# Three rotary units moved from the projection stage into the key-search score stage, and the search's state put in PSUM

## The chip, the cores and the metric

The kernel runs on one core of a Trainium2 chip. The metric is the device time of one execution in microseconds; the median of the runs counts. The engines are PE (TensorE), DVE (VectorE), ACT (ScalarE), POOL (GpSimd) and SP (which here only starts DMAs).

## What is computed

The reference is a first block (three gated recurrences and a feed-forward layer) and then a second block of two identical attention layers (`DEPTH_2 = 2`) on a sequence of 1024 tokens and a width of 1024. Only the second block is touched. Of one of its layers this matters:

```python
h = jnp.einsum('bsd,de->bse', x, w_in)          # all projections at once
sq = rope(sq...); sk = rope(sk, pos)            # queries and key of the sparse attention
iq = rope(iq...); ik = rope(ik, pos)            # queries (8 heads) and key of the index
sc = jnp.einsum('bqhd,bsd->bqhs', qib, ki)
idx_score = jnp.einsum('bqhs,bqh->bqs', jax.nn.relu(sc), wib)
idx_score = where(causal, idx_score, -inf)      # then top-k: the 256 best keys of every query
```

The sparse attention then looks only at each query's 256 best keys. The other projections (`fox` queries and keys, the gate, the `diff` queries and keys with rotary embedding, the values) do not depend on the search.

## The kernel before, in words

A **unit** is one 128-column slice of the projection, computed transposed into a PSUM pair (two banks, 128x1024): `unit_products` (L357) issues 48 matmuls, that is 2 halves x 8 row blocks `k` x `three_products` (L341, lines 344 to 346), since each f32 operand is split in a rounded part and a rest. POOL makes the split of the weights for each unit (a CAST, then a subtract of the full width). Some units are rotary: DVE takes the pair out twice (times cos into the destination, times sin into `rot`), ACT's queue starts four DMAs that turn the halves (`turn_halves`, L368) into `partner`, and DVE adds `partner` to the destination.

Each stage is an `nc.Block`: every engine has its own in-order program, semaphores order them, and all engines meet at the end of the block. One layer runs, in this order:

1. `product_stage` "pa" (L375): eight rotary units, three for `SQ` (sparse queries and key) and five for `IQ` (index queries and key), with four PSUM pairs in rotation, then a **wide** part: 332 columns of token-major products in all eight banks, of which bank pair `t//2` may be written once the unit that used it last has been taken out (`scaled`). ACT makes a rounded copy `SQ_high`, POOL the rest `SQ_rest`. DMA loads go through six slots.
2. `index_stage` (L1840): scores. For each of the eight query tiles `t` (with n = 128(t+1) keys) and each pair of the eight heads (32 **steps** in all, 64 heads `j`), PE multiplies two heads, each with 64 rows, into one of four PSUM pairs (L1866); ACT applies relu into `R`, four slots (L1878); DVE multiplies by the head's weight and adds up (L1894, L1891), and after each `t` takes the largest absolute value (L1898) and adds the causal mask (L1899). No units run here.
3. `search_stage` (L1999). DVE runs `TopK.search` (L1934): 32 rounds of bisection. A round is `mid` = `lo` + step (L1958), three counts on DVE (L1961) beside three on ACT (L1930), `keep` = count <= need (L1965), `lo` += keep x step (L1966). Then `TopK.select` (L1975) picks exactly 256 keys. Meanwhile PE computes 20 units over four PSUM pairs: 12 that ACT copies out between its counts (`COPIED`), then 8 rotary units that DVE takes out after it has finished the search and the selection. PE may start unit u when unit u-4 has been taken out. After the units comes a wide part of 512 columns in the eight banks. PE begins with five spin matmuls (L338) that keep it busy until the first weights are split.
4. The three attention stages and `finish_stage`.

The order of work on each engine is written out by hand; there is no planner.

Of the kernel before, what the change touches and what calls it, by code (L numbers as in the profile page):

```python
# [16 lines left out]
P = 128  # L17
# [357 lines left out]
def product_stage(kit, tag, XT, rest, items, ropes, rope, place, rot, partner, halves, wide):  # L375
# [9 lines left out]
    (products, taken, dve_own, scaled, rope_in, split, rounded, bank_done, wide_taken, high_done, low_done) = (  # L385
        kit.sem(f"{tag}_{n}") for n in ("products", "taken", "dve_own", "scaled", "rope_in", "split", "rounded",
                                        "bank_done", "wide_taken", "high_done", "low_done"))
    with ExitStack() as mem:
# [5 lines left out]
        with nc.Block() as block:  # L394
# [33 lines left out]
            @block.scalar  # L428
            def _(act):
                for n in range(U + 1):  # L430
# [5 lines left out]
                    if 0 < n <= len(halves):  # L436
                        plain, high, _ = halves[n - 1]
                        act.wait_ge(taken, n)
                        act.activation(high, plain, ACT.Copy).then_inc(high_done, 1)
# [5 lines left out]
            def _(pool):  # L445
                for i, (_, width) in enumerate(items):
# [7 lines left out]
                    if 0 <= i - 3 < len(halves):  # L454
                        plain, high, low = halves[i - 3]
                        pool.wait_ge(high_done, i - 2)
                        pool.tensor_tensor(low, plain, high.bitcast(FP32), ALU.subtract).then_inc(low_done, 1)
# [1382 lines left out]
def index_stage(kit, IQ, VS, IS, AM, causal, prepare):  # L1840
# [3 lines left out]
    scored, bent, added, done, own_d = (kit.sem(f"ix_{n}") for n in ("scored", "bent", "added", "done", "own_d"))  # L1844
    H = 8
    SLOTS = 4
    with ExitStack() as mem:
        R = sbuf(nc, mem, "ix_R", [P, SLOTS, S])
        with nc.Block() as block:
            @block.sync  # L1850
            def _(sp):
                prepare.load(sp)

            @block.tensor
            def _(pe):
                for t in range(NT):
                    n = P * (t + 1)
                    for h in range(0, H, 2):
                        j = t * H + h
                        if j >= SLOTS:  # L1860
                            pe.wait_ge(bent, j + 1 - SLOTS + 1)
                        for c in range(0, n, HALF):
                            e = min(n, c + HALF)
                            for m in range(2):
                                rows = slice(64 * m, 64 * m + 64)
                                last = pe.matmul(kit.pair((j + m) % SLOTS)[:, c:e], IQ[rows, h // 2, t * P:(t + 1) * P],  # L1866
                                                 IQ[rows, 4, c:e], start=True, stop=True)
                                if e == n:
                                    last.then_inc(scored, 1)

            @block.scalar
            def _(act):
                for j in range(NT * H):
# [4 lines left out]
                    act.activation(R[:, j % SLOTS, 0:n], kit.pair(j % SLOTS)[:, 0:n], ACT.Relu).then_inc(bent, 1)  # L1878

            @block.vector  # L1880
            def _(dve):
                own = Own(dve, own_d)
                for t in range(NT):
                    n = P * (t + 1)
                    out = IS[:, keys_at(t):keys_at(t) + n]
                    for h in range(H):
# [9 lines left out]
                        ins.then_inc(added, 1)  # L1896
                    dve.wait_ge(added, (t + 1) * H)
# [5 lines left out]
class TopK:  # L1903
# [5 lines left out]
    def __init__(self, kit, mem, IS, AM, MB, B, R, causal):  # L1909
# [6 lines left out]
        self.mid, self.cnt, self.need, self.keep, self.lo, self.hi = (  # L1916
            small(n, [P, 2 * N]) for n in ("mid", "cnt", "need", "keep", "lo", "hi"))
# [17 lines left out]
    def search(self, dve):  # L1935
# [4 lines left out]
        lo, hi, mid, keep, steps, top = self.lo, self.hi, self.mid, self.keep, self.steps, self.top  # L1940
# [4 lines left out]
        own(dve.tensor_scalar(lo, steps[:, 0:1].to_broadcast([P, 2 * N]), -1.0, None, ALU.mult))  # L1945
# [11 lines left out]
        for i in range(BISECTIONS):  # L1957
            dve.tensor_scalar(mid, lo, steps[:, i:i + 1], None, ALU.add).then_inc(self.act_mid, 1)  # L1958
# [7 lines left out]
            own.then(dve.scalar_tensor_tensor(lo, keep, steps[:, i:i + 1], lo, ALU.mult, ALU.add))  # L1966
# [32 lines left out]
def search_stage(kit, XT, rest, items, topk, staged, partner, rot, fox, GATE, FQD, rope, DQD, DV):  # L1999
# [5 lines left out]
    n_pairs, SLOTS, PARTS, RING, TURNS = 4, 2, 2, len(staged), 2  # L2005
# [7 lines left out]
    (rounded, split, products, copied, rope_in, scaled, added, dve_own, bank_done, wide_taken) = (  # L2013
        kit.sem(f"tk_{n}") for n in ("rounded", "split", "products", "copied", "rope_in", "scaled", "added",
                                     "dve_own", "bank_done", "wide_taken"))
    with ExitStack() as mem:
# [5 lines left out]
        with nc.Block() as block:  # L2022
# [10 lines left out]
            def _(pool):  # L2033
                for i, (_, width) in enumerate(items):
# [6 lines left out]
                    pool.tensor_tensor(w2, w, w1.bitcast(FP32), ALU.subtract).then_inc(split, 1)  # L2041

            @block.tensor
            def _(pe):
                spin(kit, pe, 3, 5)
# [9 lines left out]
                for k in range(KT):  # L2055
                    i = U + k
                    pe.wait_ge(split, i + 1)
                    for t in range(NT):
                        if k == 0 and t % 2 == 0:
                            pe.wait_ge(scaled, ROPES - n_pairs + t // 2 + 1)  # L2060
# [5 lines left out]
                        elif t == NT - 1:  # L2066
# [3 lines left out]
            def _(act):  # L2070
# [24 lines left out]
                for t in range(NT):  # L2095
                    act.wait_ge(bank_done, t + 1)
# [754 lines left out]
def layer(kit, l, XD, XT, REST, DQ, C, LAM, OM, GATE, FQD, DQD, half_size, d):  # L2851
# [23 lines left out]
    items = [(w_feat[m], S) for m in range(8)]  # L2875
    items += rows_of(w_tok, 0, 332)
    dst = [SQ[:, j, :] for j in range(3)] + [IQ[:, j, :] for j in range(5)]
    ropes = [(dst[m], QK_SCALE if m < 2 else IDX_SCALE if 3 <= m < 7 else 1.0) for m in range(8)]
# [3 lines left out]
                  rot=MB[:, 0:4 * S].bitcast(FP32).rearrange("p (a n) -> p a n", a=2),  # L2882
                  halves=[(SQ[:, m, :], SQ_high[:, m, :], SQ_rest[:, m, :]) for m in range(3)], wide=wide)
    IS = flat[:, 0:KEYS]
    index_stage(kit, IQ, VS, IS, AM, causal, prepare)
    index.close()
    DV = ends.enter_context(nc.sbuf_tensor("DV", [P, NT, 512], FP32, side="right"))[:, :, :]
    with ExitStack() as mem:
# [5 lines left out]
        search_stage(kit, XT, REST, items, topk, staged, slots_of(0, 2), slots_of(2, 4), [QK_SCALE] * 2 + [1.0] * 2, GATE, FQD, rope, DQD, DV)  # L2894
# [146 lines left out]
```

## Time and profile before

| | |
|---|---|
| median of 3 runs | 3120.19 us (3117.55 to 3122.45) |
| the profiled execution | 3115.68 us, its span 3114.0 us |
| PE busy | 2840.1 us, 91% of the span |
| DVE busy | 1677.7 us, 54% |
| ACT busy | 983.8 us, 32% |
| POOL busy | 791.7 us, 25% |

The times of the trace count from the start of the span. The two layers lie at 1349 to 2216 us and from 2234 us on. A matmul of 512 columns is shown with 0.39 us, though the next one starts 0.23 us later: they overlap, so the distance between starts is what a matmul costs. "Idle" in brackets is the time the engine stood still before the row, and behind the arrow what released it.

### The profile page before, as it was taken

What the parts mean: (1) busy time and instruction counts of PE and PEld (TensorE: products, weight loads), DVE (VectorE), ACT (ScalarE), POOL (GpSimd) and SP (SyncE); (2) the same over time, 40 slices, a digit from 0 to 9 for tenths busy, and PEclk for the clock granted to TensorE, in tenths of its full rate; (3) what the DMA queues carried; (4) which work ended last, traced back from release to release, by engine and by line L of the source; (5) the groups of instructions that cost most, each with busy time, mean ns of one, the idle gap of its engine ahead of it and who ended that gap; (6) DMA issues with size and microseconds to landing.
All of it is one profiled execution on the core that took longest, in us unless ns stands there. A gap on an engine that the chain in (4) does not pass through costs nothing. (4 is left out here: it accounts for less than half of the span.)

```text
span 3114.0 us, 39179 instructions
## 1 busy us (share of the span) xinstructions
PE 2840.1 (91%) x14936; PEld 2311.2 (74%) x14936; DVE 1677.7 (54%) x2806; ACT 983.8 (32%) x1911; POOL 791.7 (25%) x510
## 2 busy tenths in 40 slices
PE   6999888989999999989699889989897898999988
PEld 4768678778888888868388778777684686778767
DVE  5170476534223233333999545675446998265855
ACT  3150454220000000111564034563105560244751
POOL 2233103223233333323033261003130332340021
PEclk9999899999999999999999999999899999999999
DMA  3101002111111111131122420004320224300032
GB/s 113 35 34 49 1 1 99 48 41 38 51 58 38 50 59 48 55 122 47 41 89 89 139 92 1 1 13 165 131 64 3 96 87 123 141 1 1 1 135 95
DMA packets 83146, 194.07 MB, mean 62 GB/s; under 512 B 15488, under 2 KB 34448, under 8 KB 81936
## 3 DMA queue, kind: packets, MB, share of 16 engines
q1 hardware_dynamic: 71056, 153.78, 14.6%
q10 hardware_dynamic: 11904, 37.76, 3.9%
q8 instruction: 123, 2.02, 0.3%
q14 instruction: 63, 0.52, 0.1%
HBM read 141.18 MB, written 33.55 MB: 56 GB/s over the span
## 5 line engine op out<-in xcount | busy, mean ns | idle before, releaser
L344 PE MATMUL psum<-H,tk_W 128*128 128x512 f32 x640 | 250.9, 392 | 23.1 <-DVE OM L2124 22.9
L344 PE MATMUL psum<-H,ffn_W 128*128 128x512 f32 x672 | 262.9, 391 | 4.8 <-DVEq L1716 3.1
L346 PE MATMUL psum<-H,ffn_W 128*128 128x512 f32 x672 | 262.4, 390 | 0.0
L345 PE MATMUL psum<-H,ffn_W 128*128 128x512 f32 x672 | 262.4, 390 | 0.0
L345 PE MATMUL psum<-H,tk_W 128*128 128x512 f32 x640 | 250.3, 391 | 0.0
L346 PE MATMUL psum<-H,tk_W 128*128 128x512 f32 x640 | 250.0, 391 | 0.0
L1930 ACT ACTIVATE MB<-OM,tk_mid 128x384 bf16<-128x384 f32 (+2 forms) x192 | 157.2, 819 | 120.7 <-DVE tk_mid L1958 119.9
L1961 DVE TENSOR_SCALAR_CACHE_REDUCE MB<-OM,tk_mid 128x512 bf16<-128x512 f32 (+2 forms) x192 | 184.3, 1010 | 2.3
L1483 POOL CAST ffn_W<-ffn_W 128x1024 fp32r<-128x1024 f32 (+1 forms) x77 | 65.1, 845 | 471.4 <-PE psum L346 469.6
L2039 POOL CAST tk_W<-tk_W 128x1024 fp32r<-128x1024 f32 (+1 forms) x56 | 53.6, 958 | 512.1 <-PE psum L346 361.0
L1697 DVE TENSOR_SCALAR ffn_Y<-ffn_G,ffn_par 128x1024 f32<-128x1024 f32 x21 | 21.1, 1004 | 288.6 <-ACT ffn_G L1670 288.6
L1670 ACT ACTIVATE ffn_G<-psum 128x1024 f32<-128x1024 f32 x21 | 21.6, 1029 | 445.6 <-PE psum L346 445.6
L344 PEld LDWEIGHTS psum<-H,tk_W 128*128 128x128 f32 x640 | 121.0, 189 | 50.1 <-issue 23.7
L1485 POOL TENSOR_TENSOR ffn_W<-ffn_W,ffn_W 128x1024 fp32r<-128x1024 f32 (+1 forms) x77 | 152.6, 1982 | 6.2
L344 PEld LDWEIGHTS psum<-H,ffn_W 128*128 128x128 f32 x672 | 126.8, 189 | 32.3 <-POOLq L1556 3.5
L346 PEld LDWEIGHTS psum<-H,ffn_W 128*128 128x128 f32 x672 | 126.7, 189 | 26.7
L345 PEld LDWEIGHTS psum<-H,ffn_W 128*128 128x128 f32 x672 | 126.8, 189 | 26.1
L2715 POOL TENSOR_TENSOR fin_W_rest<-fin_W 128x2048 fp32r<-128x2048 f32 x4 | 22.4, 5604 | 462.8 <-ACT fin_W L2685 462.8
L346 PEld LDWEIGHTS psum<-H,tk_W 128*128 128x128 f32 x640 | 121.0, 189 | 25.4
L345 PEld LDWEIGHTS psum<-H,tk_W 128*128 128x128 f32 x640 | 121.0, 189 | 25.3
L344 PE MATMUL psum<-ffn_W,ffn_PR 128*128 128x512 f32 x336 | 131.1, 390 | 0.0
L346 PE MATMUL psum<-ffn_W,ffn_PR 128*128 128x512 f32 x336 | 130.8, 389 | 0.0
(442 smaller groups left out, 7219.7 us busy)
## 6 DMA issues: line engine op xcount, KB each, us to landing
tk_W<-in_w_feat SPq DMA_DIRECT2D x40, 512.0 KB, 3.6
ffn_W<-in_ffn_w_gate SPq DMA_DIRECT2D x21, 512.0 KB, 3.5
ffn_W<-in_ffn_w_val SPq DMA_DIRECT2D x21, 512.0 KB, 3.5
ffn_W<-in_ffn_w_down SPq DMA_DIRECT2D x42, 256.0 KB, 2.6
OM<-in_w_feat SPq DMA_DIRECT2D x16, 512.0 KB, 7.7
OM<-MB ACTq DMA_DIRECT2D x64, 128.0 KB, 2.4
GATE<-OM ACTq DMA_DIRECT2D x16, 512.0 KB, 2.9
OM<-OM ACTq DMA_DIRECT2D x64, 128.0 KB, 2.9
```

What stands on the lines that cost most here:

```text
L344: pe.matmul(out, a1, b1, start=start, stop=False)
L345: pe.matmul(out, a1, b2, start=False, stop=False)
L346: return pe.matmul(out, a2, b1, start=False, stop=stop)
L1483: pool.tensor_copy(w1, w).then_inc(self.rounded, 1)
L1485: pool.tensor_tensor(w2, w, w1.bitcast(FP32), ALU.subtract).then_inc(self.split, 1)
L1670: act.activation(G[:, j % 2, 2:2 + S], kit.pair(j % 2), ACT.Copy).then_inc(gate_out, 1)
L1697: own.then(dve.tensor_scalar(y, x[:, 2:2 + S], par[:, 2, j:j + 1], par[:, 3, j:j + 1], ALU.mult, ALU.add))
L1930: last = act.activation(self.MB[:, self.keys(t)], self.IS[:, self.keys(t)], ACT.Sign, scale=-1.0, bias=self.mid[:, 3 + n:4 + n], accum_out ...
L1961: own(dve.tensor_scalar(MB[:, self.keys(t)], IS[:, self.keys(t)], mid[:, n:n + 1], 0.0, ALU.is_lt, ALU.add, accum_out=self.cnt[:, n:n + 1]))
L2039: pool.tensor_copy(w1, w).then_inc(rounded, 1)
L2715: pool.tensor_tensor(w_part(W2, c, 0), w_part(W, c, 0), w_part(W1, c, 0).bitcast(FP32), ALU.subtract).then_inc(w_low_pool, 1)
```

## The change

- `product_stage` "pa" computes only the five `IQ` units. Its wide part waits at each bank pair for the last of the five units that used it; `SQ_high` and `SQ_rest` are no longer made here.
- `index_stage` also computes the three `SQ` units. SP loads their weights (two slots) and the cos/sin table, POOL splits them, PE cuts each unit in 16 **chunks** of three matmuls and issues some after each step (more in later tiles, none in the last four steps), all into the fourth PSUM pair; scores use three pairs. DVE takes each unit out after the second head of the step in which it ends (`rotate`, which waits for `products`), ACT's queue starts the turning DMAs four heads later, DVE adds the partner eight heads later. PE may begin unit u only when DVE has taken out unit u-1 (`scaled`).
- `search_stage` has three PSUM pairs for units; the last pair's bank 7 holds the bisection's `need` and `low` (the running lower bound, copied to `lo` in SBUF once the rounds are over). The wide part starts with banks 4 to 7. POOL now makes both `SQ_high` (in ACT's place) and `SQ_rest`, behind its splits 3, 4 and 5.

```diff
 def product_stage(...)                       # pa
-                            pe.wait_ge(scaled, U - n_pairs + t // 2 + 1)
+                            pe.wait_ge(scaled, [u for u in range(U) if u % n_pairs == t // 2][-1] + 1)
...
-                        act.activation(high, plain, ACT.Copy).then_inc(high_done, 1)
...
-                        pool.tensor_tensor(low, plain, high.bitcast(FP32), ALU.subtract).then_inc(low_done, 1)
 def index_stage(...)
-    SLOTS = 4
+    H, SLOTS, PAIRS, PARTS, UNIT_PAIR, CHUNKS = 8, 4, 3, 2, 3, 2 * KT
+    share = [j // 4 + 1 for j in range(STEPS - 4)]
+    upto = [min(CHUNKS * U, CHUNKS * U * sum(share[:j + 1]) // sum(share)) for j in range(STEPS)]
+    last_step = [[j for j in range(STEPS) if upto[j] >= CHUNKS * (u + 1)][0] for u in range(U)]
...
+                for i, (src, _) in enumerate(items):
+                    if i >= PARTS:
+                        sp.wait_ge(split, i - PARTS + 1)
+                    sp.dma_start(W[:, i % PARTS, :], src).then_inc(w_in[i % PARTS], 16)
+                    if i == 0:
+                        sp.dma_start(table, rope).then_inc(rope_in, 16)
...
+                    if i >= PARTS:
+                        pool.wait_ge(products, i - PARTS + 1)
+                    pool.tensor_copy(w1, w).then_inc(rounded, 1)
+                    pool.wait_ge(rounded, i + 1)
+                    pool.tensor_tensor(w2, w, w1.bitcast(FP32), ALU.subtract).then_inc(split, 1)
...
+                def chunk(n):
+                    u, c, k = n // CHUNKS, n % CHUNKS // KT, n % KT
+                    if n % CHUNKS == 0:
+                        pe.wait_ge(split, u + 1)
+                        if u:
+                            pe.wait_ge(scaled, u)
+                    w1, w2 = (a[:, u % PARTS, k * P:(k + 1) * P] for a in (W1, W2))
+                    at = slice(c * HALF, (c + 1) * HALF)
+                    last = three_products(pe, kit.pair(UNIT_PAIR)[:, at], w1, w2, XT[:, k, at], rest[:, k, at],
+                                          k == 0, k == KT - 1)
...
+                for step in range(STEPS):
+                    scores(step)
+                    for n in range(upto[step - 1] if step else 0, upto[step]):
+                        chunk(n)
...
+                    for u in range(U):
+                        if j == 2 * last_step[u] + 1 + SLOTS:
+                            act.wait_ge(scaled, u + 1)
+                            if u:
+                                act.wait_ge(turned, u)
+                            turn_halves(act, partner, rot, swapped)
...
+                        for u in range(U):
+                            if j == 2 * last_step[u] + 1:
+                                rotate(u)
+                            if j == min(2 * last_step[u] + 1 + 2 * SLOTS, NT * H - 1):
+                                add_partner(u)
 class TopK
+        self.need, self.low = (kit.psum[:, 7, 8 * n:8 * n + 2 * N] for n in range(2))
...
-            dve.tensor_scalar(mid, lo, steps[:, i:i + 1], None, ALU.add).then_inc(self.act_mid, 1)
+            dve.tensor_scalar(mid, low, steps[:, i:i + 1], None, ALU.add).then_inc(self.act_mid, 1)
...
             own.then(dve.tensor_tensor(keep, self.cnt, self.need, ALU.is_le))
-            own.then(dve.scalar_tensor_tensor(lo, keep, steps[:, i:i + 1], lo, ALU.mult, ALU.add))
+            own.then(dve.scalar_tensor_tensor(low, keep, steps[:, i:i + 1], low, ALU.mult, ALU.add))
+        own.then(dve.tensor_copy(lo, low))
 def search_stage(...)
-    n_pairs, SLOTS, PARTS, RING, TURNS = 4, 2, 2, len(staged), 2
+    n_pairs, SLOTS, PARTS, RING, TURNS = 3, 2, 2, len(staged), 2
+    WIDE_ORDER = (4, 5, 6, 7, 0, 1, 2, 3)
...
+                    if 0 <= i - 3 < len(halves):
+                        plain, high, low = halves[i - 3]
+                        pool.tensor_copy(high, plain).then_inc(high_done, 1)
+                        pool.wait_ge(high_done, i - 2)
+                        pool.tensor_tensor(low, plain, high.bitcast(FP32), ALU.subtract).then_inc(low_done, 1)
```

## Rows read from the trace of the kernel before

**Rows 1.** Busy by stretch, layer 1, "pa" and scores: PE, PEld, DVE, ACT, POOL, clock

```profile
1349.60:1473.00 123.40, 122.44 (x586) 103.31 (x586) 33.99 (x24) 6.28 (x10) 45.87 (x35) 0.99 0.30 88
1473.00:1539.00 66.00, 40.33 (x193) 16.44 (x192) 57.70 (x80) 41.44 (x66) 0.00 (x0) 0.91 0.01 3
```

**Rows 2.** Timeline, DVE in the score stage: start, us, line, operation, count

```profile
1475.00 3.09 DVE L1891 SCALAR_TENSOR_TENSOR OM<-ix_R,VS,OM 128x128 f32<-128x128 f32 x7
...
1516.61 8.69 DVE L1891 SCALAR_TENSOR_TENSOR OM<-ix_R,VS,OM 128x896 f32<-128x896 f32 x7
...
1538.41 0.29 DVE L1899 TENSOR_TENSOR OM<-OM,CONST 128x128 f32<-128x128 f32 x1
```

**Rows 3.** Timeline, PE in the score stage and at the search stage's start

```profile
1473.79 0.71 PE L1866 MATMUL psum<-IQ 64*128 64x128 f32 x8 [0.79 <-PEq L394]
...
1499.94 1.56 PE L1866 MATMUL psum<-IQ 64*128 64x512 f32 x8 [1.15 <-ACT ix_R L1878]
...
1526.46 1.99 PE L1866 MATMUL psum<-IQ 64*128 64x512 f32 x8 [0.52 <-ACT ix_R L1878]
1539.26 7.02 PE L338 MATMUL psum<-CONST 128*128 128x512 f32 x10 [10.81 <-PEq L1849]
```

**Rows 4.** Timeline, end of DVE's select and PE's restart, layer 1; PE's in layer 2

```profile
1730.34 1.21 DVE L2124 SCALAR_TENSOR_TENSOR OM<-psum,tk_table 128x1024 f32<-128x1024 f32 x1
...
1731.70 0.77 PE L344 MATMUL psum<-H,tk_W 128*128 128x512 f32 x1 [10.83 <-DVE OM L2124]
...
1735.56 0.39 PE L344 MATMUL psum<-H,tk_W 128*128 128x512 f32 x1
...
2616.08 0.76 PE L344 MATMUL psum<-H,tk_W 128*128 128x512 f32 x1 [12.04 <-DVE OM L2124]
```

**Rows 5.** PE alone by stretch: stretch, busy, granted clock, DMA share, GB/s

```profile
1731.70:1733.00 1.30, 1.30 (x3) 0.50 0.22 50
```

**Rows 6.** Timeline, POOL's first split in each stage and two later ones

```profile
1357.08 1.04 POOL L451 CAST pa_W<-OM 128x1024 fp32r<-128x1024 f32 x1 [0.31 <-DMA OM<-in_w_feat]
...
1542.99 1.04 POOL L2039 CAST tk_W<-tk_W 128x1024 fp32r<-128x1024 f32 x1 [75.61 <-DMA tk_W<-in_w_feat]
...
1655.73 1.04 POOL L2039 CAST tk_W<-tk_W 128x1024 fp32r<-128x1024 f32 x1 [7.35 <-PE psum L346]
...
1666.61 1.04 POOL L2039 CAST tk_W<-tk_W 128x1024 fp32r<-128x1024 f32 x1 [7.36 <-PE psum L346]
```

**Rows 7.** Timeline, rounds of the search on DVE, with one POOL row

```profile
1541.76 0.22 DVE L1958 TENSOR_SCALAR tk_mid<-tk_lo,tk_steps 128x6 f32<-128x6 f32 x1
...
1547.48 2.44 DVE L1958 TENSOR_SCALAR tk_mid<-tk_lo,tk_steps 128x6 f32<-128x6 f32 x1
...
1547.51 2.39 POOL L2041 TENSOR_TENSOR tk_W<-tk_W 128x1024 fp32r<-128x1024 f32 x1
...
1553.42 0.23 DVE L1958 TENSOR_SCALAR tk_mid<-tk_lo,tk_steps 128x6 f32<-128x6 f32 x1
...
1557.14 0.23 DVE L1958 TENSOR_SCALAR tk_mid<-tk_lo,tk_steps 128x6 f32<-128x6 f32 x1
...
1684.26 0.23 DVE L1966 SCALAR_TENSOR_TENSOR tk_lo<-tk_keep,tk_steps,tk_lo 128x6 f32<-128x6 f32 x1
```

**Rows 8.** Timeline, a wide DVE operation of the selection and POOL beside it

```profile
1711.35 2.39 POOL L2041 TENSOR_TENSOR tk_W<-tk_W 128x1024 fp32r<-128x1024 f32 x1
...
1711.67 3.02 DVE L1990 SCALAR_TENSOR_TENSOR OM<-OM,tk_lo,MB 128x896 bf16<-128x896 f32 x1
```

**Rows 9.** Groups of DVE instructions by form: a small one that reads PSUM

```profile
L2462 DVE TENSOR_REDUCE df_nmax<-psum 128x1 f32<-128x128 f32 x16 | 3.9, 285 | 2.6 <-PE psum L2391 2.6
```

**Rows 10.** Timeline, PE from 64-row to 128-row matmuls in an attention stage

```profile
1923.06 0.40 PE L2139 MATMUL psum<-FQ_high,FQ_rest 64*128 64x512 f32 x2
1923.38 0.39 PE L2221 MATMUL psum<-FB,pickb 128*128 128x512 bf16 x1
```

**Rows 11.** Timeline, ACT's queue starting the four turning DMAs of a unit

```profile
1739.44 2.45 ACTq L372 DMA_DIRECT2D OM<-OM  x4
```

More of the change, by code:

```diff
@@ L372, in turn_halves, with product_stage @@
         act.dma_start(partner[dst, :], rot[src, :]).then_inc(done, 16)
-def product_stage(kit, tag, XT, rest, items, ropes, rope, place, rot, partner, halves, wide):
+def product_stage(kit, tag, XT, rest, items, ropes, rope, place, rot, partner, wide):
     nc = kit.nc
@@ L1854, in _ @@
             @block.tensor
             def _(pe):
[L1856 to L1869, printed above, removed]
+                def chunk(n):
[8 more added lines that the diff above has]
+                                          k == 0, k == KT - 1)
+                    if n % CHUNKS == CHUNKS - 1:
+                        last.then_inc(products, 1)
@@ new lines, in scores @@
+                def scores(step):
+                    t, h = step * 2 // H, step * 2 % H
+                    n, j = P * (t + 1), 2 * step
+                    if j + 1 >= PAIRS:
+                        pe.wait_ge(bent, j + 1 - PAIRS + 1)
+                    for c in range(0, n, HALF):
+                        e = min(n, c + HALF)
+                        for m in range(2):
+                            rows = slice(64 * m, 64 * m + 64)
+                            last = pe.matmul(kit.pair((j + m) % PAIRS)[:, c:e], IQ[rows, h // 2, t * P:(t + 1) * P],
+                                             IQ[rows, 4, c:e], start=True, stop=True)
+                            if e == n:
+                                last.then_inc(scored, 1)
@@ L1882, in _, with rotate, add_partner @@
                 own = Own(dve, own_d)
+                def rotate(u):
+                    dst, scale = ropes[u]
+                    out = kit.pair(UNIT_PAIR)
+                    dve.wait_ge(products, u + 1)
+                    if u == 0:
+                        dve.wait_ge(rope_in, 16)
+                    else:
+                        dve.wait_ge(swapped, 64 * u)
+                    own(dve.scalar_tensor_tensor(dst, out, scale, cos, ALU.mult, ALU.mult))
+                    dve.scalar_tensor_tensor(rot, out, scale, sin, ALU.mult, ALU.mult).then_inc(scaled, 1)
+                def add_partner(u):
+                    dst = ropes[u][0]
+                    dve.wait_ge(swapped, 64 * (u + 1))
+                    own.wait()
+                    dve.tensor_tensor(dst, dst, partner, ALU.add).then_inc(turned, 1)
                 for t in range(NT):
@@ L1939, in search @@
         own = Own(dve, self.own_d)
-        lo, hi, mid, keep, steps, top = self.lo, self.hi, self.mid, self.keep, self.steps, self.top
+        hi, mid, keep, steps, top = self.hi, self.mid, self.keep, self.steps, self.top
+        low, lo = self.low, self.lo
         own.then(dve.tensor_reduce(top, AM[:, T0:NT], AX.X, ALU.max))
@@ L1944, in search @@
         own.then(dve.tensor_scalar(steps[:, 0:1], top, 2.0, None, ALU.mult))
-        own(dve.tensor_scalar(lo, steps[:, 0:1].to_broadcast([P, 2 * N]), -1.0, None, ALU.mult))
+        own(dve.tensor_scalar(low, steps[:, 0:1].to_broadcast([P, 2 * N]), -1.0, None, ALU.mult))
         for b in range(5):
@@ L2893, in layer @@
         items += rows_of(w_tok, 332, 844)
-        search_stage(kit, XT, REST, items, topk, staged, slots_of(0, 2), slots_of(2, 4), [QK_SCALE] * 2 + [1.0] * 2, GATE, FQD, rope, DQD, DV)
+        search_stage(kit, XT, REST, items, topk, staged, slots_of(0, 2), slots_of(2, 4),
+                     [(SQ[:, m, :], SQ_high[:, m, :], SQ_rest[:, m, :]) for m in range(3)], [QK_SCALE] * 2 + [1.0] * 2, GATE, FQD, rope, DQD, DV)
     gates = ExitStack()
```

67 lines of the change are left out of this document (36 added, 31 removed).

## The prediction, made before the changed kernel was run

> **What bounds the kernel now.** I began with the busy shares of the small table: PE is the bound in most stages, so PE work is worth moving only to where PE waits. The busy times by stretch show such a place: in the score stage's 66 us DVE is busy 57.7 and PE 40.3 [rows 1], and DVE's timeline there runs without a gap, a head of one tile taking from 0.44 us (3.09 / 7) at t = 0 to 1.24 (8.69 / 7) at t = 6, about 0.133 more per t [rows 2]. DVE ends at 1538.70; PE has been done since 1528.5 [rows 2, 3]. The second place is inside the search stage, found in the timeline around PE's longest waits: after 16 units PE stands 10.83 us in layer 1 and 12.04 in layer 2, until DVE, done with the selection, has taken out the first rotary unit [rows 4]. It restarts at a granted clock of 0.50, the lower of its two levels [rows 5], after 10.8 us of idling: nine matmuls take 3.86 us where nine at 0.227 take 2.04 [rows 4]. So DVE's search and selection set when the last units run. A unit costs PE 10.88 us, the distance of two POOL splits that each wait for one [rows 6], and a chunk of three matmuls 10.88 / 16 = 0.68.
>
> **Search state in PSUM.** The three small operations take about 0.2 us each, but one that meets a POOL instruction lasts until POOL is done: `mid` took 2.44 us from 1547.48 while POOL's subtract ran from 1547.51 to 1549.90 [rows 7]. A round that meets none takes 1557.14 - 1553.42 = 3.72; 32 of them 119.0. The search took 1684.49 - 1541.76 = 142.7 [rows 7]. If the operations no longer meet POOL, DVE is done 23.7 us earlier per layer. A wide operation with two SBUF operands also waits (3.02 us at 1711.67, about 2.1 of it behind POOL's subtract [rows 8]), so the selection keeps its collisions; it slides by 23.7 us against splits that come each 10.88, and I leave its length as it is. Price of PSUM operands: a small operation of 128 columns out of PSUM takes 0.285 us [rows 9], one within SBUF 0.29 [rows 2]: nothing. For a small write into PSUM no row exists; bounds: 0, and 0.065 per operation. I take 0, since rows 9 and 2 agree to 5 ns.
> The Trainium skill ("SBUF — State Buffer", Who interferes with whom) says that DVE shares a second port pair with GpSimd, and that an instruction with at most one SBUF input, outside the two-port modes, does not contend; by this rule all three new forms escape. The Trainium skill speaks against the change in "VectorE: DVE Perf Modes" (The TRN2 errata): 120 cycles of fixed cost out of PSUM against 58 from SBUF, an estimated 0.065 us each, 6.2 us per layer over 96 operations; the trace, with 0.285 against 0.29, disagrees. By it the sum would be about 10 us less favourable.
>
> **Three pairs instead of four.** PE now stops after 15 units instead of 16. In layer 1 it gets there at 1731.70 - 10.83 - 10.88 = 1710.0; DVE has released it at 1731.55 - 23.7 = 1707.9. Layer 2: 2593.2 against 2592.2 [rows 4, 6]. So neither waits, by 2.1 and 1.0 us. The gain is 10.83 + 12.04 and twice 1.8 for the slow restart: **-26.5 us** for both layers. It is all there is to have: a still faster DVE would find PE busy. POOL's extra work (`SQ_high` and `SQ_rest`, 3 x 3.4 us) fits in its idle 7.35 us per unit [rows 6]; it would cost if it met small operations still held. ACT's copies come, as now, between its counts.
>
> **Units out of "pa".** -3 x 10.88 = -32.6 us per layer on PE, which is busy for 122.4 of the stage's 123.4 us [rows 1]. The wide part now finds its first pair just finished by unit 4 and waits for DVE's two operations of 1.2 us: +2.4. SQ's rounding there was beside PE: nothing.
>
> **Units into the score stage.** PE's own work: scores of a step take 1.99 - 0.28 = 1.71 us at t = 7 and 0.213 less per t (1.56 at t = 5) [rows 3], 31 us in all, and 32.6 of chunks: 63 us, as much as the stage is long. So it can't be hidden whole. I follow DVE through it:
> - The first chunk sits behind step 2, with all later scores queued behind it. In the search stage the first CAST starts 3.7 us after PE's first matmul and the split is done after 7.2 [rows 3, 6]; the second follows at once, table or not (0.31 us of waiting in "pa" [rows 6]). Here: 1481.0, and POOL's second subtract holds DVE to 1484.6. Head 6 started at 1477.2 [rows 2]: **+7.4**. A clock dip like that of rows 5 hits PE, not DVE, here.
> - Unit 0 ends in step 15. Its end releases POOL's third split (3.4 us), which meets the last heads: **+3.4** (0 if it lies in a gap). DVE then takes the unit out: **+2.3**. Chunk 16 waits for that, and the scores of step 16 are queued behind it: chunk 0.68, scores 1.35, a relu of 0.63 (41.44 / 66 [rows 1]), minus 1.0 of DVE's reduce: **+1.8**, and **+1** for a slow clock.
> - Steps 16 to 22 are PE's: 15 chunks and six scores are 17.3 us, plus 14 changes between 64-row and 128-row matmuls at 0.09 (0.32 between starts instead of 0.23 [rows 10]). DVE needs 15.2 for the same heads: **+2.3**, which hides adding the partner.
> - Unit 1 ends in step 22: taken out **+2.3**, refill without cover 0.68 + 1.56 + 0.8: **+3.1**. Steps 23 to 27, by the same reckoning 16.0 against 12.9: **+3.1**. Unit 2: taken out **+2.3**, partner **+1.1**; step 28's scores are not held up.
> The sum is +30.1 us per layer. Lower bound 22 (no collision, little refill, DVE nearly as slow as PE), upper 38 (ACT's queue takes 2.45 us to start four DMAs [rows 11], twice while DVE has no heads in store; slow clocks at both refills). The Trainium skill ("TensorEngine Tiling (Array Packing)", Key Properties) says that a change of tiling mode drains PE; rows 10 show 0.09 us, so the sum stands.
>
> **Sum** per layer for the move: -32.6 + 2.4 + 30.1 = -0.1. Both layers and the search: -26.7 us. The profiled execution took 3115.7, so 3089.0 for one like it; the median of the runs shown is 4.5 us above it: **3093.5 us**. In short, PE work moved from a full stage to one that fills up, while the gain comes from the search's wait.
>
> **Rivals.**
> - *Score stage hides the units.* If DVE stays the bound after the first weights, it grows by 7.4 + 3 x (2.3 + 1.1), less what overlaps, some 16.4 us. Then -13.8 per layer more: -54.1, **3066 us**. For it: PE has 26 us without work there [rows 1]. Against it: unit u+1's chunks wait for DVE with all scores behind them.
> - *Score stage grows more,* by 40 us: late weights, ACT's DMA starts, a halved clock after each wait. Then +9.8 per layer: -6.9, **3113 us**.
> - *Slower: the lock stays.* If the operations still wait for POOL (each reads or writes one SBUF operand, and `mid` still writes to SBUF), the change doesn't do what it says: DVE releases PE when it did, PE stops one unit earlier, at +10.88 us per layer. 21.8 - 0.2: **3142 us**. It decides the sign where the search gets less than 10.9 us shorter per layer. Against it: only POOL's overlap explains why most operations take 0.2 us and a few 2.4 [rows 7].
>
> **Chances.** Forecast with its own range 3077 to 3109: 0.60; units hidden 0.18; stage grows more 0.12; lock stays 0.10. The range reaches to the first two rivals: 3066 to 3113. A measurement can tell 0.2% here, 6 us. Slower: 0.10 less a small part where the stage hides the units, 0.08; within 0.2%: half of the third case, 0.06; faster 0.86.
>
> **What would show it.** In the changed profile: `mid`, `keep` and low's update all near 0.2 us, none at 2.4, rounds at 3.72; PE's wait for L2124's successor gone or under 3 us, and the restart's slow matmuls with it; the search stage some 12 to 14 us shorter; "pa" 30 us shorter; the score stage near 96 us, with DVE's first gap of some 5 us before head 6, gaps of 2 to 3 us after the takings-out of units 0 and 1, and PE waiting for DVE in steps 15 and 22. I am wrong if the score stage is under 85 or over 106 us, if small operations still last as long as POOL, or if PE waits in the search stage for the pair of its sixteenth unit.

## The result, and the profile after

The changed kernel takes 3129.32 us (median of 17 runs, 3121.86 to 3141.86), the kernel before 3118.36 (17 runs, 3116.66 to 3126.31): ratio 1.0031, 95% interval 1.0021 to 1.0041. It is **slower by 0.31%**, some 10 us, where 26.7 us less had been forecast (3093.5, with a range of 3066 to 3113). The profiled execution took 3131.07, its span 3129.4.

Cut by PE's first instruction of each part, in us, layer 1 / layer 2:

| part | before | after | difference | forecast |
|---|---|---|---|---|
| "pa" with its spins | 124.21 / 122.66 | 95.85 / 94.07 | -28.4 / -28.6 | -30.2 |
| score stage | 65.47 / 65.45 | 111.47 / 111.67 | **+46.0 / +46.2** | **+30.1** |
| search stage | 282.43 / 283.43 | 269.55 / 269.63 | -12.9 / -13.8 | -12.6 / -13.8 |

These six differences come to +8.5 us. The spans differ by 15.4: another 5.9 lie in layer 2 behind the search and 1.4 ahead of layer 1, less 0.5 between the layers. The change touches none of these.

**The search stage** is as forecast. Groups of instructions over both layers, after:

```profile
L344 PE MATMUL psum<-H,tk_W 128*128 128x512 f32 x640 | 249.4, 390 | 0.9 <-POOL tk_W L2112 0.9
...
L2035 DVE SCALAR_TENSOR_TENSOR psum<-tk_keep,tk_steps,psum 128x6 f32<-128x6 f32 x64 | 14.6, 228 | 2.3
L2027 DVE TENSOR_SCALAR tk_mid<-psum,tk_steps 128x6 f32<-128x6 f32 x64 | 14.4, 224 | 2.2
...
L2034 DVE TENSOR_TENSOR tk_keep<-tk_cnt,psum 128x6 f32<-128x6 f32 x64 | 10.3, 161 | 9.0 <-ACT MB L1998 2.5
```

DVE's timeline of the search, first and second round and the end:

```profile
1560.87 0.22 DVE L2027 TENSOR_SCALAR tk_mid<-psum,tk_steps 128x6 f32<-128x6 f32 x1
...
1564.58 0.22 DVE L2027 TENSOR_SCALAR tk_mid<-psum,tk_steps 128x6 f32<-128x6 f32 x1
...
1680.58 0.23 DVE L2035 SCALAR_TENSOR_TENSOR psum<-tk_keep,tk_steps,psum 128x6 f32<-128x6 f32 x1
```

The means over 64 are 228, 224 and 161 ns, and in the timelines of both searches none of the 192 operations lasts over 0.23 us, where [rows 7] has 2.44. A round lasts 3.71, the search 1680.81 - 1560.87 = 119.9 us instead of 142.7, and PE's 10.83 and 12.04 us of waiting [rows 4] have become 0.9 over both layers, for weights.

**The score stage** is where the time went. Busy by stretch, after (columns as in [rows 1]: PE, PEld, DVE, ACT, POOL, granted clock, DMA share, GB/s):

```profile
1446.85:1558.32 111.47, 85.85 (x337) 45.11 (x337) 69.17 (x89) 38.19 (x64) 10.77 (x6) 0.87 0.14 40
...
1455.00:1466.00 11.00, 10.64 (x30) 5.41 (x30) 4.76 (x10) 2.43 (x8) 3.40 (x2) 0.50 0.23 62
1466.00:1470.00 4.00, 4.00 (x17) 2.00 (x18) 2.10 (x5) 1.53 (x4) 0.00 (x0) 0.84 0.00 0
1490.00:1495.00 5.00, 5.00 (x16) 2.83 (x15) 0.84 (x3) 1.30 (x2) 0.00 (x0) 0.54 0.00 0
1518.50:1522.00 3.50, 3.50 (x11) 1.34 (x10) 0.00 (x0) 0.05 (x1) 0.00 (x0) 0.52 0.00 0
```

and one stretch of the kernel before, near the start of its score stage:

```profile
1475.80:1479.80 4.00, 3.91 (x16) 1.87 (x16) 3.20 (x11) 2.47 (x8) 0.00 (x0) 0.57 0.11 26
```

PE was busy 40.33 of 66.00 us [rows 1] and is now busy 85.85 of 111.47. So it stood still 25.7 us before and stands still 25.6 now: a stage to which 32.6 us of chunks were moved because PE was idle there has **the same idle time as before**, and grew by all the work it was given and 13 us on top. Which waits took the place of the old ones, the groups of the stage say (the idle time before a group stands behind the last bar):

```profile
L1953 DVE SCALAR_TENSOR_TENSOR OM<-ix_R,VS,OM 128x128 f32<-128x128 f32 (+7 forms) x56 | 47.2, 842 | 35.8 <-ACT ix_R L1916 31.9
...
L344 PE MATMUL psum<-H,ix_W 128*128 128x512 f32 x48 | 23.5, 490 | 14.2 <-DVE OM L1937 8.2 <-POOL ix_W L1873 6.0
```

DVE, which ran without a gap before [rows 2], now waits 35.8 us for heads, and PE waits 14.2 us in front of chunks. PE's timeline there (start, us, what; in brackets the idle time before it):

```profile
1455.00 0.80 PE L344 MATMUL psum<-H,ix_W 128*128 128x512 f32 x1 [5.99 <-POOL ix_W L1873]
...
1460.47 1.23 PE L1899 MATMUL psum<-IQ 64*128 64x256 f32 x4
...
1463.20 1.23 PE L1899 MATMUL psum<-IQ 64*128 64x256 f32 x4
...
1489.32 0.77 PE L344 MATMUL psum<-H,ix_W 128*128 128x512 f32 x1 [4.37 <-DVE OM L1937]
...
1517.91 0.47 PE L344 MATMUL psum<-H,ix_W 128*128 128x512 f32 x1 [3.82 <-DVE OM L1937]
...
1528.08 1.77 PE L1899 MATMUL psum<-IQ 64*128 64x512 f32 x8
1529.79 0.50 PE L344 MATMUL psum<-H,ix_W 128*128 128x512 f32 x1
...
1531.73 0.39 PE L346 MATMUL psum<-H,ix_W 128*128 128x512 f32 x1
1532.05 1.77 PE L1899 MATMUL psum<-IQ 64*128 64x512 f32 x8
```

and DVE's beside it:

```profile
1457.72 1.60 DVE L1953 SCALAR_TENSOR_TENSOR OM<-ix_R,VS,OM 128x128 f32<-128x128 f32 x2 [7.48 <-ACT ix_R L1916]
...
1482.09 1.60 DVE L1953 SCALAR_TENSOR_TENSOR OM<-ix_R,VS,OM 128x512 f32<-128x512 f32 x2 [0.35 <-ACT ix_R L1916]
1484.72 2.19 DVE L1953 SCALAR_TENSOR_TENSOR OM<-ix_R,VS,OM 128x512 f32<-128x512 f32 x2 [1.02 <-ACT ix_R L1916]
...
1487.97 1.21 DVE L1937 SCALAR_TENSOR_TENSOR OM<-psum,MB 128x1024 f32<-128x1024 f32 x1
...
1494.15 0.55 DVE L1956 TENSOR_SCALAR OM<-ix_R,VS 128x640 f32<-128x640 f32 x1 [4.05 <-ACT ix_R L1916]
...
1522.80 2.15 DVE L1953 SCALAR_TENSOR_TENSOR OM<-ix_R,VS,OM 128x768 f32<-128x768 f32 x2 [5.03 <-ACT ix_R L1916]
...
1542.23 1.21 DVE L1937 SCALAR_TENSOR_TENSOR OM<-psum,MB 128x1024 f32<-128x1024 f32 x1
```

Three things are to be seen. (a) At a unit's end the two engines wait for each other in turn: PE stands 4.37 us until DVE has taken the unit out (the last of the two operations, 1487.97), scores queued behind it, and then DVE stands 4.05 us for those scores. (b) At or just after the end of each of PE's three waits in front of chunks the granted clock falls to the lower level (0.50, 0.54 and 0.52 in the stretches above); behind the first it stays there for 11 us, a step of t = 1 taking 1463.20 - 1460.47 = 2.73 us. The kernel before also has such a stretch (0.57), but shorter, and with DVE as the bound it cost little. (c) Even at full clock a step costs more than its parts: at t = 6 the distance is 1532.05 - 1528.08 = 3.97 us, where scores alone take 1.99 - 0.28 - 0.21 = 1.50 [rows 3] and nine matmuls 2.04. Going back to 64 rows is the smaller part of the rest: 1532.05 - 1531.73 = 0.32 us instead of 0.23.

That scores have three PSUM pairs instead of four is not the cause here: PE waited for ACT (that is, for a free pair) 4.4 us in the stage, and 3.3 of these lie in the last three steps, where DVE works without a gap.

### The profile page after: what moved, and what is told of

It reads as the page before. It is cut to its first block and busy times, and to the rows that moved or that the text cites. A ratio compares the mean times of both kernels' runs of the same rounds, so it can differ in the third digit from the quotient of the medians.

```text
span 3129.4 us, 39201 instructions
## 1 busy us (share of the span) xinstructions
PE 2869.0 (92%) x14936; PEld 2319.1 (74%) x14936; DVE 1632.4 (52%) x2808; ACT 972.3 (31%) x1905; POOL 800.1 (26%) x516
## 5 line engine op out<-in xcount | busy, mean ns | idle before, releaser
L344 PEld LDWEIGHTS psum<-H,ffn_W 128*128 128x128 f32 x672 | 126.9, 189 | 32.1 <-POOLq L1548 3.5
L1953 DVE SCALAR_TENSOR_TENSOR OM<-ix_R,VS,OM 128x128 f32<-128x128 f32 (+7 forms) x112 | 94.5, 844 | 71.7 <-ACT ix_R L1916 63.8
L344 PE MATMUL psum<-ffn_W,ffn_PR 128*128 128x512 f32 x336 | 131.2, 391 | 0.0
```

The source lines that it names most:

```text
L344: pe.matmul(out, a1, b1, start=start, stop=False)
L1953: ins = dve.scalar_tensor_tensor(out, R[:, j % SLOTS, 0:n], VS[:, t, 64 + h:65 + h], out, ALU.mult, ALU.add)
```

## The experiments

All were run beside the kernel before; the ratios are to it. "Growth" is the score stage's length in the profiled execution less 65.5 us, layer 1 / layer 2; the changed kernel's is 46.0 / 46.2. One profiled execution stands behind each pair of growths, so only the two layers show their spread, some 3 us at most.

**1. The search part alone.** State in PSUM and three pairs; all eight units stay in "pa".

```diff
+        self.need, self.low = (kit.psum[:, 7, 8 * n:8 * n + 2 * N] for n in range(2))
...
-    n_pairs, SLOTS, PARTS, RING, TURNS = 4, 2, 2, len(staged), 2
+    n_pairs, SLOTS, PARTS, RING, TURNS = 3, 2, 2, len(staged), 2
+    WIDE_ORDER = (4, 5, 6, 7, 0, 1, 2, 3)
```

> The kernel before with only the search part of the change: need and low in PSUM bank 7, three PSUM pairs for units, the wide part beginning with banks 4 to 7; all eight units stay in the projection stage. My theory (the search part gives what was forecast, the score stage eats it): the search stage is 12 to 14 us shorter per layer, the time is 24 to 28 us less than before, some 3092 us. Rival (taking the three units along is what makes the search part possible, or the search's gain is eaten elsewhere): less than 10 us.

Measured: 3098.91 against 3124.91 us, ratio 0.9913 (0.9896 to 0.9929): -26 us, the term of the prediction. The search stages took 269.59 and 269.47. From the groups of its DVE instructions:

```profile
L1968 DVE SCALAR_TENSOR_TENSOR psum<-tk_keep,tk_steps,psum 128x6 f32<-128x6 f32 x64 | 14.6, 228 | 2.3
L1960 DVE TENSOR_SCALAR tk_mid<-psum,tk_steps 128x6 f32<-128x6 f32 x64 | 14.3, 224 | 2.2
```

**2. The units alone.** State in SBUF with four pairs, as before; the three units in the score stage.

```diff
-    n_pairs, SLOTS, PARTS, RING, TURNS = 3, 2, 2, len(staged), 2
+    n_pairs, SLOTS, PARTS, RING, TURNS = 4, 2, 2, len(staged), 2
-            own.then(dve.scalar_tensor_tensor(low, keep, steps[:, i:i + 1], low, ALU.mult, ALU.add))
+            own.then(dve.scalar_tensor_tensor(lo, keep, steps[:, i:i + 1], lo, ALU.mult, ALU.add))
```

> The changed kernel with the search part undone: state in SBUF, four pairs for units, the wide part in its old order; the three units stay in the score stage. My theory: the move alone costs 46 - 28.5 us per layer as the changed trace shows, plus nothing in the search stage (PE waits 11 to 12 us there again), so some 32 to 38 us more than before, 3150 to 3157 us. Rival (the score stage's growth comes from something the two parts do together): within 10 us of the changed kernel.

Measured: 3168.42 us, ratio 1.0143 (1.0128 to 1.0159), +43.5. "pa" -28.2 / -28.2, score stage +44.8 / +43.3, and the search stage +3.9 / +4.2. 32 to 38 us more had been expected, with nothing for the search: POOL's rounding of `SQ` now lies in the search, where operations on SBUF still meet it. `lo`'s update lasted 589 ns on average there, 485 before, which is 6.7 us over 64 of them. Parts 1 and 2 together are +17.5, the whole change +11. The difference of 6.5 is about what this meeting costs, and the whole change does not have it.

**3. Three pairs without the PSUM state.** The prediction's rival "the lock stays", built.

```diff
-    n_pairs, SLOTS, PARTS, RING, TURNS = 4, 2, 2, len(staged), 2
+    n_pairs, SLOTS, PARTS, RING, TURNS = 3, 2, 2, len(staged), 2
```

> The kernel before with three pairs for units in the search stage, and the search's state left in SBUF. My theory: PE stops one unit earlier and is released when it was, 10.9 us per layer, 3138 to 3142 us. Rival (the pair matters less, because the weights' splits and ACT's copies hold PE anyway): under 10 us more than before.

Measured: 3146.91 us, ratio 1.0072 (1.0059 to 1.0086), 22.0 us over the kernel before, where 21.8 follow from two times 10.9. (The profiled execution, at 3134.22, was the shortest of five; its search stages are 7.1 and 10.4 us longer than before.) From its groups of DVE instructions:

```profile
L1958 DVE TENSOR_SCALAR tk_mid<-tk_lo,tk_steps 128x6 f32<-128x6 f32 x64 | 33.9, 530 | 2.2
L1966 DVE SCALAR_TENSOR_TENSOR tk_lo<-tk_keep,tk_steps,tk_lo 128x6 f32<-128x6 f32 x64 | 28.8, 451 | 2.2
```

Means of 530 and 451 ns against 224 and 228 in experiment 1, whose only other difference is where `need` and `low` lie. With three pairs the placement is worth 48 us; three pairs alone cost 22.

**4. Chunks behind every second step**, to halve the number of mode changes (PE going from 64-row score matmuls to 128-row chunks and back).

```diff
+    upto = [upto[j - (j + 1) % 2] if j else 0 for j in range(STEPS)]
```

> The changed kernel, with the chunks issued after every second step only (the same chunks, so 14 fewer changes from 64-row scores to 128-row chunks and back per layer). Theory 'mode changes': each step that has chunks pays some 0.4 us for its two changes; 13 to 14 fewer give 5 us per layer, 8 to 11 us less than the changed kernel. Theory 'waits and slow clock' (PE waits for the first weights and for DVE at unit ends, and runs at half clock behind): no difference beyond 3 us, or slower because a burst of chunks delays the scores.

Measured: 3148.98 us, ratio 1.0072 (1.0052 to 1.0091); growth 51.7 / 48.8, more than with the change as it is, where 5 us less had been expected. Two steps of scores in a row have only three pairs: PE's waits for ACT went from 4.4 to 13.2 us in the stage. That may hide what fewer changes gave; the run decides nothing on their price.

**5. Late start**: the first chunk behind step 8 (counted from 0), when its weights are long there.

```diff
-    share = [j // 4 + 1 for j in range(STEPS - 4)]
+    share = [j // 4 + 1 if j >= 8 else 0 for j in range(STEPS - 4)]
```

> The changed kernel, with no chunk in the first eight steps (t = 0 and 1), so that PE does not stand before the first weights with all later scores queued behind it; the 48 chunks are spread over steps 8 to 27 in the same proportion. Theory 'wait at the start' (PE waits 6.0 us for the first weights, DVE 7.5 us, and PE then runs at a granted clock of 0.50 for 12 us): the score stage is 6 to 10 us shorter per layer, 12 to 20 us less than the changed kernel. Rival 'PE's work is the bound' (the chunks only move to later steps, where PE is the bound): under 6 us in all.

Measured: 3124.71 against 3120.26 us, ratio 1.0013 (1.0002 to 1.0025); growth 44.1 / 44.0. PE's wait of 5.99 us is gone and only 2 us with it, where 6 to 10 had been expected. PE's timeline of this kernel shows the other half of the start's price still there:

```profile
1450.64 0.49 PE L1899 MATMUL psum<-IQ 64*128 64x128 f32 x4 [0.36 <-ACT ix_R L1916]
1451.49 1.22 PE L1899 MATMUL psum<-IQ 64*128 64x256 f32 x4 [0.36 <-ACT ix_R L1916]
```

1.22 us for four matmuls is the lower clock, though PE had waited for 0.79 us once and then for no more than 0.36 at a time. The chunks left out early come back as more chunks in later steps, where PE is the bound as well.

**6. Spins while PE waits for the first weights**, into the pair of the units.

```diff
                 def chunk(n):
                     u, c, k = n // CHUNKS, n % CHUNKS // KT, n % KT
+                    if n == 0:
+                        spin(kit, pe, UNIT_PAIR, 7)
```

> The changed kernel with seven spin matmuls (about 6 us of PE's work at the full clock) between the scores of step 2 and the first chunk, where PE waits for weights; nothing else. Theory 'slow clock': the granted clock is back at 1.00 when the chunks begin, instead of 0.50 up to 1467 us, and the score stage is 4 to 6 us shorter per layer, 8 to 12 us in all. Theory 'wait and work' (the clock matters little, as DVE sets the pace in the first tiles): within 3 us of the changed kernel.

Measured: 3125.24 us, ratio 1.0009 (0.9997 to 1.0020); growth 41.4 / 42.5, so the slow clock behind the first wait was worth 4.6 and 3.7 us (4 to 6 had been expected). It is less in layer 2, where the clock dipped during the spins themselves: they took 7.97 us there and 6.28 in layer 1. The first scores of t = 1 in its timeline of layer 1, to be held against the 1.22 of experiment 5:

```profile
1458.90 0.70 PE L1901 MATMUL psum<-IQ 64*128 64x256 f32 x4 [0.36 <-ACT ix_R L1918]
```

**7. Two steps without chunks behind each unit**, so that no chunk waits for DVE and scores flow while it takes the unit out.

```diff
-    upto = [min(CHUNKS * U, CHUNKS * U * sum(share[:j + 1]) // sum(share)) for j in range(STEPS)]
+    upto = [0, 0, 1, 1, 2, 3, 4, 5, 6, 7, 9, 10, 12, 14, 16, 16, 16, 18, 20, 22, 25, 28, 32, 32, 32, 36, 40, 44, 48, 48, 48, 48]
```

> The changed kernel with two chunk-free steps after the end of units 0 and 1 (which end in steps 14 and 22), and unit 2's chunks in steps 25 to 28; so that PE puts scores in store while DVE catches up and takes the unit out. Theory 'in-order wait at the unit ends' (PE waits 4.37 and 3.82 us for DVE, and DVE then 4.05 and 5.03 us for scores): both kinds of gap shrink to under 2 us, the stage is 5 to 9 us shorter per layer, 10 to 18 us in all. Rival 'PE's work is the bound' (what PE gains there it pays in the fuller steps after): under 6 us in all.

Measured: 3106.63 us, ratio 0.9954 (0.9938 to 0.9970), by the two ratios some 24 us less than the changed kernel; growth 34.8 / 32.1, more of a gain than the 5 to 9 us expected. Groups and stretch of its score stage:

```profile
L344 PE MATMUL psum<-H,ix_W 128*128 128x512 f32 x48 | 22.3, 465 | 6.0 <-POOL ix_W L1873 6.0
```
```profile
1446.48:1546.76 100.28, 80.80 (x337) 43.58 (x337) 69.62 (x89) 38.19 (x64) 10.63 (x6) 0.91 0.15 44
```

The 8.2 us behind L1937 are gone, and the mean granted clock went from 0.87 to 0.91. DVE's waits for heads went from 35.8 to 27.7 us, and it goes on with stored heads right behind both takings-out.

**8. Late start and pauses together.**

```diff
-    upto = [min(CHUNKS * U, CHUNKS * U * sum(share[:j + 1]) // sum(share)) for j in range(STEPS)]
+    upto = [0, 0, 0, 0, 0, 0, 2, 4, 6, 8, 10, 12, 14, 16, 16, 16, 19, 22, 25, 28, 30, 32, 32, 32, 35, 38, 41, 44, 48, 48, 48, 48]
```

> Both schedules at once: no chunk in steps 0 to 5, two to four chunks per step from step 6 to 28, two chunk-free steps after units 0 and 1. If start and unit ends add up, the score stage is some 14 us shorter per layer than in the changed kernel (near 97 us instead of 111.5) and the time some 28 us less, near the time of the search part alone plus 4. If PE's work is the bound, the stage stays above 105 us.

Measured: 3092.97 against 3120.26 us, ratio 0.9915 (0.9896 to 0.9934); growth 28.7 / 27.0: 17.3 and 19.2 less than the changed kernel, more than the two schedules gave singly (1.9 + 11.2 and 2.2 + 14.2). Its score stage by stretch and by groups:

```profile
1447.27:1541.42 94.15, 79.12 (x336) 43.34 (x337) 74.35 (x89) 38.30 (x64) 10.72 (x6) 0.93 0.16 47
```
```profile
L344 PE MATMUL psum<-H,ix_W 128*128 128x512 f32 x48 | 21.7, 452 | 0.4 <-POOL ix_W L1873 0.4
```

PE now stands still 94.15 - 79.12 = 15.0 us instead of 25.6: this schedule fills that much of its idle time and no more. "pa" is 28.2 and 28.6 us shorter in this kernel, so the move is worth next to nothing even so (+0.5 and -1.6 us); the whole gain is the search's.

**9 and 10. Two units, and one unit, in the score stage**, the rest in "pa"; experiment 9 starts in step 6 and pauses two steps after its first unit, experiment 10 has one chunk behind each of the steps 8 to 23. The cut is experiment 10's; experiment 9 has `range(1)` there.

```diff
-    items = [(w_feat[3 + m], S) for m in range(5)] + rows_of(w_tok, 0, 332)
+    items = [(w_feat[m], S) for m in range(2)] + [(w_feat[3 + m], S) for m in range(5)] + rows_of(w_tok, 0, 332)
```

> The changed kernel with only two units in the score stage (SQ's first is back in the projection stage), one or two chunks per step from step 6 to 28, a pause of two steps after the first. Theory 'one chunk per step is nearly free, the next ones are not': a step has 1.1 to 1.3 us between PE's scores and DVE's heads, of which its two mode changes take 0.4 and a chunk 0.68. Then the stage grows by 14 to 18 us per layer (weights' splits, two takings-out, the steps with two chunks) and the projection stage shrinks by 20 to 22: some 5 us per layer less than the search part alone, 3080 us. Rival 'the stage's growth goes with PE's work alone': 19 us more in the score stage, within 4 us of the search part alone.

> The same with one unit, one chunk in each of the steps 8 to 23. Theory 'one chunk per step is nearly free': the score stage grows by 4 to 7 us per layer (the taking-out and the partner 3.4, the split's collision with DVE 2 to 3.4), the projection stage shrinks by 10.9: some 4 to 6 us per layer less than the search part alone, 3080 to 3084 us. Rival 'the growth goes with PE's work': 9 to 11 us more in the score stage, no gain over the search part alone.

| units moved | growth | "pa" | ratio (interval) |
|---|---|---|---|
| 0 (experiment 1) | 0 / 0 | +0.1 / +0.6 | 0.9913 (0.9896 to 0.9929) |
| 1 | 10.6 / 9.3 | -9.9 / -9.7 | 0.9928 (0.9910 to 0.9947) |
| 2 | 18.0 / 18.9 | -19.5 / -19.7 | 0.9909 (0.9887 to 0.9932) |
| 3 (experiment 8) | 28.7 / 27.0 | -28.2 / -28.6 | 0.9915 (0.9896 to 0.9934) |

A unit costs the score stage 9.0 to 10.6 us, and "pa" gives 9.4 to 9.9 for it. The theory of both, that one chunk behind a step is nearly free, fell: growths of 14 to 18 and of 4 to 7 had been expected by it. Experiment 10's timeline shows one more price, where POOL's first split meets DVE (DVE and POOL rows):

```profile
1467.52 0.81 DVE L1953 SCALAR_TENSOR_TENSOR OM<-ix_R,VS,OM 128x128 f32<-128x128 f32 x2 [0.22 <-ACT ix_R L1916]
1468.68 3.65 DVE L1953 SCALAR_TENSOR_TENSOR OM<-ix_R,VS,OM 128x128 f32<-128x128 f32 x2 [0.36 <-ACT ix_R L1916]
...
1469.80 2.39 POOL L1873 TENSOR_TENSOR ix_W<-ix_W 128x1024 fp32r<-128x1024 f32 x1
```

Two operations take 3.65 us here; the two before them took 0.81.

**11. The price of a mode change**: experiment 8 with one chunk moved between the two column blocks of the scores in nine steps per layer. Same matmuls, one more pair of changes per such step.

```diff
                     for c in range(0, n, HALF):
                         e = min(n, c + HALF)
+                        if c and between is not None:
+                            chunk(between)
```

> The kernel with late start and pauses, but in nine steps per layer (17 to 21 and 25 to 28) one of the step's chunks is issued between the two column blocks of the scores instead of behind them: the same matmuls, two more mode changes in each of these steps. Theory 'a pair of mode changes costs 0.4 us of PE' (read off the distances of starts): the score stage is 3 to 4 us longer per layer, and within these steps the distance from the first to the last matmul's start grows by 0.4 us each. Rival (what I read off is the latency of the scores' last matmul, or waiting, and order doesn't matter): the stage stays within 1 us, the step's length is unchanged.

Measured: 3106.32 against 3123.32 us, ratio 0.9950 (0.9933 to 0.9967); growth 30.9 / 31.0, which is 2.2 and 3.9 us over experiment 8, where 3 to 4 had been expected. Steps of t = 6, first in experiment 8, then here:

```profile
1509.58 1.77 PE L1899 MATMUL psum<-IQ 64*128 64x512 f32 x8
...
1513.55 1.77 PE L1899 MATMUL psum<-IQ 64*128 64x512 f32 x8
```
```profile
1511.61 1.13 PE L1901 MATMUL psum<-IQ 64*128 64x512 f32 x4
1512.67 0.50 PE L344 MATMUL psum<-H,ix_W 128*128 128x512 f32 x1
...
1513.56 0.92 PE L1901 MATMUL psum<-IQ 64*128 64x384 f32 x4
...
1516.00 1.13 PE L1901 MATMUL psum<-IQ 64*128 64x512 f32 x4
```

1516.00 - 1511.61 = 4.39 us against 1513.55 - 1509.58 = 3.97: **0.42 us** for a change to 128 rows and back. The Trainium skill ("TensorEngine Tiling (Array Packing)", Key Properties) says that changing the tiling mode drains TensorE. It gives no price; the direction agrees, and here the price is over twice the 0.18 that the prediction took. That the extra time is a drain no run here shows.

## Why the prediction was wrong

**Search state in PSUM, three pairs: right.** All three operations became short, PE's wait and its slow restart went, and PE does not wait for the pair of its sixteenth unit. -26.5 was forecast; the stages give -12.9 - 13.8 = -26.7, and experiment 1 has -26. Experiment 3 settles the reason: with the same three pairs and the state in SBUF the small operations are held as before, at 3146.91 where the rival "the lock stays" was given 3142. The Trainium skill ("SBUF — State Buffer", Who interferes with whom) speaks of an exclusive lock that operations with at most one SBUF input escape. The trace agrees, if the one-column `steps` is not counted as an input: up to 2.45 us each before, 0.23 at most after. The Trainium skill's fixed cost out of PSUM ("VectorE: DVE Perf Modes", The TRN2 errata), by which each search would have lasted an estimated 6 us longer, is not seen: 0.22 to 0.23 us with PSUM operands, as in SBUF [rows 7].

**Units out of "pa": nearly right,** -28.4 and -28.6 against -30.2. The wait for DVE is 2.54 us in layer 1, where 2.4 was forecast; not forecast was the clock behind it, on average 0.79 from 1412 to 1420. Behind the same wait in layer 2 the clock stays at 1.00; there the stage's first 20 us, whose work is as before, show 0.86 instead of 0.93.

**Units into the score stage: the step that failed.** +30.1 per layer was forecast, with 38 as the upper bound; +46.0 was measured, beyond the 40 of the rival "score stage grows more", of whose conditions the halved clock after each wait came true. The step put DVE's path through the stage; read at the same places (layer 1, growth against the timeline of before at the same head):

| up to | forecast | measured |
|---|---|---|
| head 31's end: first weights, collision | 10.8 | 17.2 |
| head 32's start: unit 0 taken out, refill | +5.1 | +6.3 |
| head 46's start: steps 16 to 22, unit 1, refill | +7.7 | +13.8 |
| unit 2 taken out: steps 23 to 27 | +5.4 | +7.7 |
| the end | +1.1 | +1.0 |

- *First weights, +7.4.* The wait was right: head 6 started 1457.72 - 1446.85 = 10.9 us into the stage, 10.8 was forecast. Wrong was the sentence that a clock dip "hits PE, not DVE, here". With one chunk behind each step at half clock a step of t = 1 takes 2.73 us and DVE needs 1.1, so PE, not DVE, set the pace from step 3 on. Experiment 6 removes the slow clock (in layer 2 not all of it): -4.6 and -3.7.
- *Refills, +2.8 and +3.1.* I counted the one chunk and the one set of scores that DVE must wait for, not that scores of this and the next step could have been made while DVE took the unit out. DVE's own gaps are 4.05 and 5.03 us, and PE refills in them at the lower clock (0.54 and 0.52). Experiment 7 takes away the in-order wait for `scaled` at the head of PE's queue and gets back 11.2 and 14.2 us per layer, the largest part of the miss. It is more than these two terms missed by, as scores in store also cover the taking-out itself; the chunks lie in other steps too, so not all of it need be the wait.
- *Mode changes, 0.18 per step.* It is 0.42, and I charged it only from step 16 on, while 25 steps have chunks: by this price an estimated 25 x 0.42 = 10.5 us of PE's time, where 12 x 0.18 = 2.2 was charged. The price came from [rows 10], one change in one direction, from `f32` to `bf16` matmuls in an attention stage: too far away.
- *Third split's collision, +3.4.* It cost 0.6: the two heads from 1484.72 took 2.19, where the two before them took 1.60. This term was too large and hid part of the miss.
- *Slips of reckoning.* The refill's parts, 0.68 + 1.35 + 0.63 - 1.0, make 1.7, not 1.8; and 17.3 + 1.3 - 15.2 for steps 16 to 22 makes 3.4, where 2.3 was put. Neither changes the picture.

The common root is in the way of reckoning. I followed DVE and let PE in at single places, while PE was the bound from step 3 to step 27. PE's own account says it at once: 45.5 us more busy, of which 32.6 chunks; the granted clock (0.87 against 0.91) explains roughly 111.5 x 0.13 - 66 x 0.09 = 8.6 more, the remaining 4 are the mode changes less the modelled ends of the score groups, which stood alone before and are overlapped now; and 14.2 us of new waits took the place of the idle time that was to be filled. Experiment 8, in which no chunk waits for POOL or DVE for more than 0.4 us, grows by 28.7 and 27.0. That this is near my 30.1 is no merit: without its start and refill terms my sum is 16.8.

The closing test of the prediction, "wrong if the score stage is over 106 us", was the right one, and it reads 111.5. The chance of slower, 0.08, hung on the lock alone; the slowdown came another way. I had bounded the stage's growth at 40 by my own terms, though PE's order of work alone allowed more.

**Does the move pay at all?** Not in any form tried. 0, 1, 2 or 3 units, scheduled with a late start and pauses, give ratios from 0.9909 to 0.9928 whose intervals overlap; a gain or loss of some 6 us could hide in them. Experiment 1, the search part alone, is 26 us faster than the kernel before and by the ratios some 37 faster than the changed one, and the simplest of them.

**Open.** Stretches that no edit touches differ by up to 9 us between the profiled executions: from the end of layer 1's search to layer 2 it is 412.7 us before, 412.2 after, 420.9 in experiment 1. The cause was not looked for; comparisons by stage are free of it, those of whole times not. How much of the growth is mode changes was not measured: experiment 11 gives the price of one pair of changes, and the 10.5 us above are an estimate from it.

## What to carry to other kernels

Idle time of an engine in a stage is room for work only if that work never waits at the head of the engine's in-order queue: put into it a chunk that waits for a slower engine, and everything queued behind stops, the slower engine runs dry in turn, and the clock falls. Before moving work, add up the receiving engine's own time, with the changes of mode and the slow clock in it, and compare with what the stage lasts; where both are alike, the move is at best a change of place. And three six-element operations 64 times over can be worth more than 65 us of matmuls moved: look at the spread of small operations that lie beside POOL's.

## What was not expected of the hardware

- A change from 64-row to 128-row matmuls and back costs 0.42 us at full clock (experiment 11, steps of 4.39 against 3.97 us).
- The granted clock fell to 0.50 at a score stage's start though PE had waited 0.79 us once and then 0.36 at a time between short groups of 0.49 us (experiment 5, 1451.49). The kernel before shows the same (0.57 from 1475.80). With seven spin matmuls behind the third group it stayed high in layer 1 (1458.90, 0.70 us for what took 1.22).
- Six-element DVE operations with a PSUM operand take 0.16 to 0.23 us, no longer than unheld ones in SBUF (0.17 to 0.23 in the kernel before), and none of 192 was held by POOL; in SBUF their mean was 0.45 to 0.53 us for the two that were held most (experiment 3).
